# LayerNorm and gates of a convolution computed by feature beside the attention, in a fused two-block float32 kernel

## The reference, cut to what matters

```python
u = h @ w_in                      # h: 512 rows x 1024; w_in: 1024 x 2816
a_val, a_gate, q, k, v, z = split(u)   # 512, 512, 512, 128, 128, 1024 wide
y_a = silu(layer_norm(dwconv(a_val * sigmoid(a_gate)), ln_g, ln_b))  # 31 taps, 512 features
y_b = attention(q, k, v)          # 8 heads of 64, 2 key/value heads, 512 features
y = concat(y_a, y_b) * silu(z)
x = x + gate * (y @ w_out)        # w_out: 1024 x 1024
# the next layer's adaptation: shift, scale, gate = split(silu(cond) @ w_ada + b)
```

## Time and profile before

| | us |
|---|---|
| median of 3 runs | 1179.72 |
| lowest and highest run | 1179.49, 1181.21 |
| the profiled execution's own time | 1177.84 |
| span of the profiled execution | 1176.0 |
| PE busy | 1117.7 (95%) |
| DVE busy | 761.0 (65%) |
| ACT busy | 553.3 (47%) |
| mean granted TensorE clock | 0.992 |

### The profile page before, as it was taken

How to read it: one execution, slowest core, us unless ns; L and a number is a source line. 1 busy time by engine, 2 the same in 40 slices (tenths; PEclk the granted TensorE clock), 3 DMA queues, 4 the chain that set the end, 5 groups by cost and what they waited for, 6 DMA issues and landing times. The chain is left out here.

```text
span 1176.0 us, 18535 instructions
## 1 busy us (share of the span) xinstructions
PE 1117.7 (95%) x7190; PEld 962.6 (82%) x7190; DVE 761.0 (65%) x1466; ACT 553.3 (47%) x987; POOL 43.2 (4%) x54
## 2 busy tenths in 40 slices
PE   6999999999999999989999999899989899999997
PEld 5877879899887877879999898888858788988855
DVE  4575756645555475776888887699656745752475
ACT  4543735544444443845444444435457331633273
POOL 1000000000000000000000000100300000000000
PEclk9999999999999999999999999999999999999999
DMA  9558045555564557046565465332461532573101
GB/s 357 198 166 329 2 144 179 174 191 186 173 210 149 184 189 266 2 143 199 173 194 194 164 208 179 91 112 93 142 245 34 203 105 72 100 270 108 37 1 55
DMA packets 51644, 182.87 MB, mean 155 GB/s; under 512 B 17636, under 2 KB 30308, under 8 KB 31972
## 3 DMA queue, kind: packets, MB, share of 16 engines
q1 hardware_dynamic: 51556, 181.68, 46.2%
HBM read 178.78 MB, written 2.89 MB: 154 GB/s over the span
## 5 line engine op out<-in xcount | busy, mean ns | idle before, releaser
L222 DVE TENSOR_TENSOR w_lo<-ring,w_hi 128x1024 fp32r<-128x1024 f32 x260 | 317.3, 1223 | 239.7 <-ACT w_hi L216 236.9
L216 ACT CAST w_hi<-ring 128x1024 fp32r<-128x1024 f32 x260 | 271.3, 1052 | 341.5 <-PE banks L278 331.0
L278 PE MATMUL banks<-f_hi,w_hi 128*128 128x256 f32 x512 | 144.1, 281 | 0.5 <-DVE f_lo L442 0.5
L278 PE MATMUL banks<-f_hi,w_lo 128*128 128x256 f32 x512 | 143.9, 281 | 0.0
L278 PE MATMUL banks<-f_lo,w_hi 128*128 128x256 f32 x512 | 143.9, 281 | 0.0
L278 PE MATMUL banks<-w_hi,u_hi 128*128 128x512 f32 x256 | 101.2, 395 | 0.0
L278 PE MATMUL banks<-w_lo,u_hi 128*128 128x512 f32 x256 | 101.2, 395 | 0.0
L278 PE MATMUL banks<-w_hi,u_lo 128*128 128x512 f32 x256 | 101.1, 395 | 0.0
L278 PEld LDWEIGHTS banks<-f_hi,w_hi 128*128 128x128 f32 x512 | 96.5, 188 | 1.3 <-DVE f_lo L442 0.8
L278 PEld LDWEIGHTS banks<-f_lo,w_hi 128*128 128x128 f32 x512 | 96.5, 188 | 0.5
L278 PEld LDWEIGHTS banks<-f_hi,w_lo 128*128 128x128 f32 x512 | 96.5, 188 | 0.0
(11 more groups left out here) (392 smaller groups left out, 2290.1 us busy)
## 6 DMA issues: line engine op xcount, KB each, us to landing
ring<-in_w_up SPq DMA_DIRECT2D x32, 1024.0 KB, 5.1
ring<-in_w_down SPq DMA_DIRECT2D x32, 1024.0 KB, 5.1
ring<-in_w_in SPq DMA_DIRECT2D x24, 1024.0 KB, 5.2
ring<-in_ab_ada SPq DMA_DIRECT2D x12, 1024.0 KB, 5.2
ring<-in_cd_ada SPq DMA_DIRECT2D x12, 1024.0 KB, 5.2
ring<-in_cd_in SPq DMA_DIRECT2D x12, 1024.0 KB, 7.6
ring<-in_w_out SPq DMA_DIRECT2D x8, 1024.0 KB, 6.9
ring<-in_ab_in SPq DMA_DIRECT2D x16, 512.0 KB, 4.8
```

Of the source, the lines that this page charges most:

```text
L216: nc.scalar.copy(w_hi[:, n % PARTS, :], part_source(key, q)).then_inc(hi_ready, 1)
L222: nc.vector.tensor_tensor(w_lo[:, n % PARTS, :], part_source(key, q), w_hi[:, n % PARTS, :].bitcast(F32), ALU.subtract).then_inc(part_read ...
L278: mm = nc.tensor.matmul(dst, a, b, start=first_one and i == 0, stop=last_one and i == 2, skip_group_check=shares_bank)
```

## The change

- The stages `finish_conv_and_gate` and, for this layer, `turn_mixed` are gone.
- In `project_and_convolve`, k and v keep their layout, but z is computed by feature: in slab 3 beside k and v, all of slab 4, and in slab 5. ACT takes the tanh of each z chunk from PSUM and DVE gates it (`find_z_tanh`, `gate_z`, two buffers). In the middle of the last slab PE sums the convolution over its features with a matrix of constants; DVE subtracts the mean, ACT squares, DVE adds the squares up.
- `transpose_groups` gets a variance by four small products, a power on POOL, and the spread of the result over partitions by four products, copied by ACT.
- `attend` gets the rest of the LayerNorm, the silu, the gate and the hi/lo split of the convolution half as its asides.
- `out_project` transposes the attended half itself, gates and splits it while slab 0 runs, and takes the three `cd_conv` slabs of adaptation inside slab 1. `ab_out` is no longer split ahead (before, `turn_mixed` split its part 0), and its halves come before those of `cd_conv`.

Cut to its core; the removed functions are those quoted above.

```diff
-... ("cd_turn", 1), ("cd_conv", 3), ("ab_out", 2), ...
+... ("cd_turn", 1), ("ab_out", 2), ("cd_conv", 3), ...
 transpose_groups, PE:
+    for t in range(4):
+        mm = nc.tensor.matmul(banks[:, VARIANCE, 4 * t:4 * t + 4], squares[:, t * P:(t + 1) * P],
+                              minus_half[:, 0:4], start=True, stop=True)
+    mm.then_inc(summed, 1)
     ...
     adapt_products(pe, key, 0, burst_bank)
-    keep_busy(burst_bank + 1, 4)
+    pe.wait_ge(rstd_ready, 1)
+    for t in range(4):
+        mm = nc.tensor.matmul(banks[:, SPREAD, t * P:(t + 1) * P],
+                              rstd[:, 48 + t:49 + t].broadcast_to([P, P]), ident[:], start=True, stop=True)
+    mm.then_inc(spread_ready, 1)
+    keep_busy(VARIANCE, 5)
 transpose_groups, ACT, at its end:
+    act.wait_ge(spread_ready, 1)
+    nc.scalar.copy(rstd_rows, banks[:, SPREAD, :])
 out_project, PE:
+    def adapt(q):
+        if q == 1:
+            pe.wait_ge(gated, len(tiles))
+            pe.wait_ge(half_used, first["cd_conv"])
+            adapt_products(pe, "cd_conv", 0, 0)
+            turn_conditions(cd_row, banks[:, TURNED, 0:16])
+        if q == 2:
+            adapt_products(pe, "cd_conv", 1, 1)
+            adapt_products(pe, "cd_conv", 2, 2)
+            turn_row(0)
     ...
+    if attended is not None:
+        for g in range(4):
+            for t in range(4):
+                mm = nc.tensor.transpose(banks[:, 4 + g, t * P:(t + 1) * P],
+                                         mixed[:, t, BANK + g * P:BANK + (g + 1) * P], ident[:])
+            mm.then_inc(turned_here, 1)
     for s in range(2):
         multiply_slab(..., behind=... adapt if adaptation is not None and s == 1 ...)
     ...
+        turn_row(1)
+        turn_row(2).then_inc(turned, 1)
+        keep_busy(0, 5)
 out_project, ACT:
+    if attended is not None and q == 0:
+        high(0)
+    if attended is not None and q == 1:
+        for g in range(1, 4):
+            high(g)
     ...
+    for j in range(3):
+        keep_adapted(act, "cd_conv", j, j, cd_rows[:, j, :]).then_inc(kept, 1)
     split_ahead(split_hi, act, key)
 out_project, DVE:
+    if attended is not None and q == 0:
+        gate(0)
     split_own(split_lo, dve, key, q)
+    if attended is not None and q == 0:
+        gate(1)
+        low(0)
+    if attended is not None and q == 1:
+        gate(2)
+        low(1)
+        gate(3)
+        low(2)
+        low(3)
     ...
+    dve.wait_ge(half_used, first["cd_conv"] + 6)
     split_ahead(split_lo, dve, key)
     ... the four tiles of slab 1 are gated and added ...
+    dve.wait_ge(turned, 1)
+    step(add_biases(1, 2, banks[:, TURNED, 0:64], 4))
+    find_scales(1)
 project_and_convolve, PE, last slab (48 products of 512 columns in place of 96 of 256):
+        if q == 1:
+            pe.wait_ge(tap_done, n_taps)
+            pe.wait_ge(z_ready, 1)
+            for half, source in enumerate((convolved, convolved_ctx)):
+                mm = accumulate(banks[:, MEAN, half * SEQ:(half + 1) * SEQ],
+                                [(minus_half[:, 0:1].broadcast_to([P, P]), source(c)) for c in range(4)])
+            mm.then_inc(mean_ready, 1)
+    pe.wait_ge(z_ready, 6)
+    keep_busy(0, 7)
 project_and_convolve, ACT:
-    copy_products(s)           # four copies at q = 13, 17, 21 and at the end
+    q == 13: four copies; q == 17: two copies, find_z_tanh(0), (1); q == 21: find_z_tanh(2) to (5)
+    act.wait_ge(centred, 2)
+    for half in range(2): ... Square of 128 x 1024 ... .then_inc(squared, 1)
+    act.wait_ge(chunk_done, 1)
+    find_z_tanh(6)
+    products_done(act, key, KV + 2)
+    find_z_tanh(7)
 project_and_convolve, DVE (gates before the taps of the same q):
+    q == 17: gate_z(0), (1); q == 21: gate_z(2) to (5)
     ...
+    dve.wait_ge(mean_ready, 1)
+    ... two scalar_tensor_tensor of 128 x 1024, the broadcast mean in PSUM as in0 ... .then_inc(centred, 1)
+    dve.wait_ge(squared, 2)
+    ... adds of 128 x 1024 and of 128 x 512 ...
+    for n in range(6, 8):
+        gate_z(n)
 attend, asides (one step after each unit):
-    four tanhs of 1024 elements on ACT, four scalar_tensor_tensor of 1024 on DVE
+    DVE: 4 multiplies by the spread rstd; for each of 4 chunks one tensor_scalar and two
+         scalar_tensor_tensor of 512; 4 subtractions to y_lo
+    ACT: 4 tanhs of 512, 4 copies of 512 to y_hi
```

More of the change, by code:

```diff
@@ L903, in _, with out_project @@
                             op0=ALU.mult, op1=ALU.mult)
-        def out_project(key, turned_y, tiles, gates=None, ctx_hidden=None, spare=None):
+        def out_project(key, turned_y, tiles, gates=None, ctx_hidden=None, spare=None, adaptation=None,
+                        attended=None):
             beside = ctx_hidden is not None
-            with stage("gated", "tile_done", *CTX_ROW_SIGNALS, *CTX_SIGNALS) as (
-                    gated, tile_done, *signals), nc.Block() as block:
+            if adaptation is not None:
+                cd_row, cd_rows = adaptation
+                gated_y, silu_z = attended
+                y_hi, y_lo = turned_y
+            TURNED = 3
+            with stage("gated", "tile_done", "kept", "turned", "bias_step", "turned_here", "gate_done", "high_ready",
+                       "low_ready", *CTX_ROW_SIGNALS, *CTX_SIGNALS) as (
+                    gated, tile_done, kept, turned, bias_step, turned_here, gate_done, high_ready, low_ready,
+                    *signals), nc.Block() as block:
                 if beside:
@@ L916, in _ @@
                     load_behind(sp, key, 2)
+                    if adaptation is not None:
+                        load_behind(sp, "cd_conv", 3)
                 @block.tensor
@@ L1103, in row_max @@
                         return nc.vector.tensor_tensor_reduce(here, here, mask, 1.0, so_far, ALU.add, ALU.min, least)
-                    more = iter(()) if aside is None else aside(aside_step)
+                    more = iter(()) if aside is None else aside(aside_vector, aside_done)
                     for i in range(n_units + WEIGH):
@@ L2445, in second_block @@
[L2445 to L2450 removed]
+                        tanh_y = proj[:, :, BANK:2 * BANK]
@@ L2452, in second_block @@
+                        attend(units, (proj[:, 0:3, 0:BANK], sb3("probsT", [P, 2, BANK])) + sums2,
+                               finish_conv, finish_conv_scalar)
+                    out_project("ab_out", turned_y, (0, 1, 2, 3), [gate_rows[:, v, :] for v in range(2)],
+                                adaptation=(cd_row[:], proj[:, 1:4, 0:BANK]),
+                                attended=([proj[:, g, AB_Q0:AB_Q0 + BANK] for g in range(4)], silu_z[4:8]))
                 own = (0, 1)
@@ new lines, in multiply_last_gates @@
+                def multiply_last_gates(pe):
+                    hi, lo = hidden
+                    s = KV + 2
+                    for q in range(4):
+                        pe.wait_ge(part_ready, first_part[key] + 4 * s + q + 1)
+                        wh, wl = part(key, 4 * s + q)
+                        for f in range(2):
+                            for kk in range(2):
+                                k = 2 * q + kk
+                                cols = slice(f * P, (f + 1) * P)
+                                mm = multiply(banks[:, Z_BANK[6 + f], :], (wh[:, kk, cols], wl[:, kk, cols]),
+                                              (hi[:, k, :], lo[:, k, :]), k == 0, k == KC - 1)
+                            if q == 3 and f == 0:
+                                mm.then_inc(chunk_done, 1)
+                        mm.then_inc(part_used, 1)
+                        if q == 1:
[7 more added lines that the diff above has]
+                    keep_busy(0, 7)
```

340 lines of the change are left out of this document (195 added, 145 removed).

## The result

The changed kernel takes 1171.62 us (median of 6, 1168.44 to 1174.75) against 1179.74 for the kernel before (6, 1177.96 to 1181.21): a ratio of 0.9931, with the interval 0.9912 to 0.9950, so 8.1 us less where 9.6 were forecast. One further execution, at 1363.63 us and a mean clock of 0.77, was disturbed and is left out everywhere. The profiled execution took 1169.81 us with a span of 1168.0.

The account below looks back on a forecast made before the run. PE, busy 95% of the span, was taken to bound the kernel, with time to win where it served DVE's serial chain. 5.3 + 0.95 + 0 - 26.84 + 10.97 = -9.6 us, against the median 1179.72: 1170.1 us, range 1166.5 to 1175.5.

Parts of the forecast that it names:

- the serial chain: DVE's LayerNorm and gates between attention and output projection, served by PE; removing both stages was to save 26.8 us.
- The projection, +5.3: Last slab: PE waits 1.1 us for taps, mean takes 3.4, and the chain over DVE and ACT ends the stage.
- The slack on parts 16 to 21: Projection: 3.2 us of slack cover DVE's extra 1.4 us at q = 17; cost nothing, without slack up to 1.4.
- `transpose_groups`, +0.95: Eight added instructions before the transposes, 0.95 us; bounds 1.2 less at full clock, 0.7 more at low.
- The attention, 0: New asides make DVE 1.67 us a unit, under PE's 1.885, so PE sets the pace; bounds -0.5 to +2.
- the slower rival: Attention becomes DVE's: unhidden asides, 20 steps of 0.62, lengthen it by 12.4 us; 1182.5 us, chance 0.04.
- The removed stages and `out_project`, -15.9: Both stages between attention and output projection go, -26.84 us; the output projection grows by 10.97 through moved work.
- The bound of "a few us": `out_project`: the last half of `cd_conv`, issued at t + 36.3 and needed at t + 46, is covered, else a few us.
- The rival of the clock: Clock falls in `out_project`, at slab 0 and the next layer's start: 1173.5; also behind both adaptations: 1177; chance 0.17.
- DVE was not late in the projection: Rival: DVE's new gates delay splits beyond the slack, PE waits in slabs 4 and 5, at most 4 us: 1174; chance 0.08.
- The moved work was not free: Rival: mean's tail hidden or better clock in `transpose_groups`, 2 to 3 us less, 1167.5; cheaper moved work, chance 0.09.

Follow-up runs that it names:

- mean_late: Changed kernel with the mean's products behind part 22 of the last slab instead of part 21: 1174.96 us (0.9964).
- the split ahead: Edit to the changed kernel: part 0 of `ab_out` is split as the attention's last aside; run by itself 1179.56 us (1.0000).
- again_2: The changed kernel itself once more, unedited: 1173.06 us (0.9930).
- mean_early: Changed kernel with DVE's last four taps before the gates and the mean's products behind part 20: 1172.09 us (0.9930).
- order_alone: Changed kernel with only `out_project`'s end reordered: ACT rounds the next slab before copying the last rows, DVE splits before waiting for adaptation: 1173.34 us (0.9942).
- the repeats: Two more sets of the unedited changed kernel: 1173.04 us (0.9946) and 1173.06 us (0.9930).
- asides_after: Changed kernel with the attention's 20 aside steps run after the last unit instead of spread over the units: 1184.03 us (1.0037).
- best2: Changed kernel with taps first, mean behind part 20, `out_project`'s end reordered and the extra products of `busy`: 1170.72 us (0.9921).
- early_end: Changed kernel with taps first, mean behind part 20 and `out_project`'s end reordered, without extra products: 1170.22 us (0.9927).
- busy: Changed kernel with wider variance products in `transpose_groups`, and more kept-busy products ending `out_project` (four) and the heads (two): 1170.52 us (0.9916).
- ahead_alone: Changed kernel with only the split of `ab_out`'s part 0 moved into the attention's last steps: 1179.56 us (1.0000).

## Why the prediction was right, and where it wasn't

It forecast 1170.1 us (1166.5 to 1175.5), faster; 1171.62 was measured, and 1173.04 and 1173.06 later. Its mechanism held: the serial chain leaves PE's path, and about 17 of its 26.8 us come back as the work named. That the sum came so close, -10.0 in the profiled stretch against -9.6, is partly luck. The profiled execution had no fall of the clock in `transpose_groups`, and this hid the 1.0 us by which the attention was missed; with the usual 9.7 us there the sum would be -8.3.

- **The projection, +5.3: measured +5.0, by the steps named.** PE waited for the taps (0.64 us, forecast 1.1). The mean took 853.40 - 850.03 = 3.37 us for 16 instructions, 0.211 each, where the forecast had 3.4. The issue gap that the Trainium skill gives for one isolated product ("TensorE: Matmul & The Clock Gate", Back-to-back issue gap), 0.109 us for 256 columns, would by estimate have made it 0.9 us; these float32 products took 0.42 us each, nearly four times that. The chain ended the stage, and `mean_late` moved its end by exactly as much as it moved the mean. The slack on parts 16 to 21 held: there is no wait of PE in those slabs.
- **`transpose_groups`, +0.95.** The first profile says -0.4, 0.13 below the lower bound given (-0.25: no fall of the clock). By the usual 9.7 us it is +1.2, inside the bounds (upper end +1.65), and by the three profiles over 11 us +2.6 to +2.9, outside. The eight added instructions took 0.88 us (872.54 to 873.42, forecast 0.95). So the step stood and the clock's share was bounded too tightly: how long it is low varies more than the one profile before could show.
- **The attention, 0: this step failed, by 1.0 us.** "PE still sets the pace" is right for the middle (3.77 a pair, to the hundredth), and the slower rival (DVE sets it) didn't come. The 0 was drawn from that middle alone. The asides also stand in the units with which the pipeline fills and empties, and there a late minimum on DVE makes PE late; that is the 0.3 and 0.65 found above. The bounds (-0.5 to +2) cover the size, but they had only the filling as a reason, not the emptying.
- **The removed stages and `out_project`, -15.9: measured -15.5.** Slab 0 began 2.54 us after the transposes (forecast 2.65), the first adaptation at 35.4 (35.3), the scales ended at 57.5 (57.2), the next layer came at 58.3 (58.0). The bound of "a few us" for the late half of `cd_conv` wasn't needed. A turned row was priced at 0.95 us; its own rows give 933.35 - 932.44 = 0.91, and two rows at the end took 986.05 - 984.35 = 1.70. It changes little here, since DVE and not PE ends the stage.
- **The rival of the clock, given 0.17, was half true.** The clock stayed at 1.00 before slab 0 in every profile without the split ahead and with the asides in their place, but at the next layer's start it fell in several (`again_2`, `mean_early`, `order_alone`), for the 1.7 us priced, and in `mean_early` for twice that (988 to 995). In no profile did it fall behind the adaptations inside slab 1. With the attention's 1.0 one such fall would make up most of the gap between the forecast and the repeats: 1170.1 + 1.0 + 1.7 = 1172.8. This is an account that fits, not one that is shown, since only one execution of each kernel was profiled. The forecast treated the clock as the kernel's; it is the execution's, so a median must carry a share of it.
- **The other rivals.** DVE was not late in the projection. The moved work was not free. That the saving hangs on hiding the moved work is seen in `asides_after`: with its asides unhidden, the changed kernel is slower than the kernel before.

## What to carry to other kernels

A pace read from the middle of a software pipeline prices work put into it only there. Here the steps in the middle cost nothing, and those in the units that fill and empty the pipeline cost 1.9 us, so price these apart, or keep asides out of them. An aside may wait for another engine only if that wait is over when its turn comes: one 1.23 us subtraction, queued behind ACT, cost 4.6 us in the attention and brought 0.85 in the stage that it came from. And where a stage ends by a chain over three engines, as this projection does, look at the place of the chain's first step before the amount of work around it.

## What the runs showed of the hardware

- The granted clock differs between executions of one program at one place. Idle times of about 1 us at the borders between stages were followed by 3 to 7 us at half clock in most profiles and by none in others, as above. In 19 executions of the changed kernel the time spreads over 9.6 us (1168.22 to 1177.86), and it follows the mean clock (0.997 to 0.990). The kernel before spreads nearly as far (1177.23 to 1184.84), which is why the 2 to 3 us of the best edits can't be told from zero.
- Extra products at two borders left the median where it was (`best2` 1170.72, `early_end` 1170.22) and cost 0.9 us themselves at the end of `out_project`. Whether they make the time steadier is open: the spread was 1.6 us in `best2` and 4.9 in `busy`.
- A wait in dense work can cost twice: in `ahead_alone` 2.69 us of waiting of PE made the attention 4.6 us longer. The clock's means of 0.63 and 0.51 behind it (928 to 932) account for 1.7 of that.
